# Prompt values taken for two heads in turn, later conditioning products, and half of the gate weights on another queue

## The reference

```python
def adaln_terms(c, w_ada, b_ada):
    mod = jax.nn.silu(c) @ w_ada + b_ada
    return tuple(m[:, None, :] for m in jnp.split(mod, 6, axis=-1))

def merge_branches(oa, ob, ga, gb, w_pa, w_pb, w_o):
    b, s = oa.shape[:2]
    ya = oa.reshape(b, s, A_OUT) @ w_pa
    yb = ob.reshape(b, s, B_OUT) @ w_pb
    return (ga * ya + gb * yb) @ w_o

def decoder_layer(x, c, pos, p, attend):
    sh1, sc1, gt1, sh2, sc2, gt2 = adaln_terms(c, p['w_ada'], p['b_ada'])
    h = rmsnorm(x, p['g_pre_mix']) * (1 + sc1) + sh1
    qa, ka, va, qb, kb, vb, logf, ga, gb = mixer_inputs(h, p['w_in'], p['b_f'], pos)
    oa, ob, state = attend(qa, ka, va, qb, kb, vb, logf)
    mix = merge_branches(oa.astype(x.dtype), ob.astype(x.dtype), ga, gb, p['w_pa'], p['w_pb'], p['w_o'])
    x = x + gt1 * rmsnorm(mix, p['g_post_mix'])
    h2 = rmsnorm(x, p['g_pre_ffn']) * (1 + sc2) + sh2
    ffn = hier_moe(h2, p['w_rg'], p['b_rg'], p['w_re'], p['b_re'], p['w_eg'], p['w_eu'], p['w_ed'])
    x = x + gt2 * rmsnorm(ffn, p['g_post_ffn'])
    return x, state
```

## Time and profile before

| | before |
| --- | --- |
| median of 3 runs | 1123.67 us (1120.25 to 1128.92) |
| the profiled execution | 1123.34 us, span 1121.2 us |
| PE busy (share of the span) | 984.8 us (88%) |
| VectorE / ScalarE / GpSimd busy | 384.2 / 206.1 / 186.8 us |
| DMA | 349.32 MB, mean 312 GB/s |
| mean granted TensorE clock | 0.949 |

### The profile page before, as it was taken

How to read it: one execution, slowest core, us unless ns; L and a number is a source line. 1 busy time by engine, 2 the same in 40 slices (tenths; PEclk the granted TensorE clock), 3 DMA queues, 4 the chain that set the end, 5 groups by cost and what they waited for, 6 DMA issues and landing times.

```text
span 1121.2 us, 17873 instructions
## 1 busy us (share of the span) xinstructions
PE 984.8 (88%) x7308; PEld 579.4 (52%) x7308; DVE 384.2 (34%) x889; ACT 206.1 (18%) x505; POOL 186.8 (17%) x210
## 2 busy tenths in 40 slices
PE   6999999998799999889999898699969997777860
PEld 4444444444467756666667565345545554444430
DVE  4200033215686373854057313115521320010005
ACT  4000000003354211002100212113312211111114
POOL 0000043302120103222230111000023332122110
PEclk9999999999899899989999999899969999899995
DMA  9997776687867699999999885997489999999956
GB/s 297 407 333 267 265 264 249 244 284 244 277 228 268 222 306 354 347 364 321 380 346 341 311 288 195 371 351 296 194 306 365 373 373 391 385 381 395 411 217 253
DMA packets 101805, 349.32 MB, mean 312 GB/s; under 512 B 11642, under 2 KB 59650, under 8 KB 82782
## 3 DMA queue, kind: packets, MB, share of 16 engines
q1 hardware_dynamic: 80414, 261.50, 65.1%
q0 software_dynamic: 15552, 79.97, 19.6%
q10 hardware_dynamic: 5760, 6.72, 1.9%
HBM read 336.31 MB, written 63.36 MB: 356 GB/s over the span
## 4 chain that ended last, share of the span: by engine, by line
PE 37%; DMA 22%; DVE 4%; issue 1%; ACT 1%; SPq 1%; DVEq 0%; POOLq 0%; ACTq 0%
DMA w_all<-in_w_exp 15%; PE bank L1665 9%; PE bank L2273 5%; PE bank L2104 5%; DMA w_all<-in_w_gates 3%; PE bank L1603 3%; PE bank L1657 2%; PE bank L1541 2%; PE bank L2124 2%; PE bank L1655 1%; DVE mods L1787 1%; PE bank L1526 1%; DMA turned<-in_w_o 1%; PE bank L1588 1%; PE bank L1569 1%
## 5 line engine op out<-in xcount | busy, mean ns | idle before, releaser
L1665 PE MATMUL bank<-turned,w_all 128*128 128x320 f32 (+1 forms) x512 | 145.0, 428 | 9.2 <-DMA w_all<-in_w_gates 3.9
L485 PE MATMUL bank<-w_all,turned 128*128 128x481 f32 (+2 forms) x384 | 120.3, 504 | 1.4 <-DVE turned L736 1.3
L485 PE MATMUL bank<-w_ring,turned 128*128 128x481 f32 (+2 forms) x384 | 118.4, 502 | 0.0
L1665 PEld LDWEIGHTS bank<-turned,w_all 128*128 128x128 f32 x512 | 95.0, 195 | 44.9 <-issue 20.0
L2104 PE MATMUL bank<-w_all,mix_row 128*64 128x256 f32 x736 | 95.2, 417 | 25.3 <-DMA w_all<-in_w_exp 24.3
L2104 PEld LDWEIGHTS bank<-w_all,mix_row 128*64 128x64 f32 x736 | 62.6, 151 | 64.8 <-issue 44.1
L1787 DVE STREAM_TRANSPOSE mods<-w_all 128x2048 f32<-128x2048 f32 (+1 forms) x39 | 86.3, 2236 | 22.2 <-PE bank L1541 9.1
L485 PEld LDWEIGHTS bank<-w_ring,turned 128*128 128x128 f32 (+1 forms) x384 | 57.2, 172 | 60.4 <-issue 57.3
L485 PEld LDWEIGHTS bank<-w_all,turned 128*128 128x128 f32 (+1 forms) x384 | 56.5, 172 | 61.6 <-issue 58.3
L2150 DVE COPY act_t<-bank 128x128 f32<-128x128 f32 x33 | 9.6, 291 | 199.4 <-PE bank L2114 197.7
L746 DVE COPY w_all<-bank 128x481 f32 (+5 forms) x32 | 16.9, 531 | 152.0 <-PE bank L485 151.8
(11 more groups left out here) (357 smaller groups left out, 1282.5 us busy)
## 6 DMA issues: line engine op xcount, KB each, us to landing
w_all<-in_w_exp SPq DMA_DIRECT2D x22, 2048.0 KB, 40.0
out_a_sample<-in_cache_a SPq DMA_DIRECT2D x8, 4080.0 KB, 21.9
w_all<-in_w_exp SPq DMA_DIRECT2D x25, 1024.0 KB, 37.6
mods<-in_w_ada SPq DMA_DIRECT2D x18, 1024.0 KB, 7.5
w_all<-in_cache_a SPq DMA_DIRECT2D x22, 512.0 KB, 7.3
turned<-in_w_exp SPq DMA_DIRECT2D x5, 2048.0 KB
mods<-in_w_exp SPq DMA_DIRECT2D x5, 2048.0 KB, 42.7
w_all<-in_cache_a SPq DMA_DIRECT2D x36, 256.0 KB, 5.8
```

Source lines behind the costliest of these rows:

```text
L485: mm = nc.tensor.matmul(m.banks[i][r:r + ROWS[i], 0:hi - lo], m.hT[:, k, i * P:i * P + ROWS[i]], ring[u][:, CW * k + lo:CW * k + hi], star ...
L1665: mm = nc.tensor.matmul(GATE[:, 0:WIDTH[h]], gate_w[b][k][:, c % 2 * P:(c % 2 + 1) * P], m.hT[:, k, 256 * h:256 * h + WIDTH[h]], start=k = ...
```

## The change

Three things change. In `weigh` of an A job the loop over the two heads becomes the innermost. The conditioning products, two of which lie ahead of the jobs, get none in the first three jobs, and the rest are spread over the other 21. In `phase_c` the first piece still runs ahead of step 0, but pieces 1 to 39 run one step later than before; and the second gate's weights of pairs 1 to 3 are loaded by ScalarE, at its step after the last reading piece, and no longer by SyncE.

```diff
-        OPENING = 2
-        pieces_at = lambda n: range(OPENING + (PIECES - OPENING) * n // N, OPENING + (PIECES - OPENING) * (n + 1) // N)
+        OPENING, FROM = 2, 3
+        upto = lambda n: OPENING + (PIECES - OPENING) * max(n - FROM, 0) // (N - FROM)
+        pieces_at = lambda n: range(upto(n), upto(n + 1))
...
-                    for b in range(2):
-                        h = 2 * p + b
-                        out = OUT[64 * b:64 * b + 64, i * P:(i + 1) * P]
-                        for x in range(min(i, 1) + 1):
-                            c = VA + HD * h
-                            nc.tensor.matmul(out, m.qkv[:, i - x, c:c + HD], pt[:, n % 2, b, x * P:(x + 1) * P], start=x == 0, stop=False)
-                        for g in range(2):
-                            for r in range(4):
-                                mm = nc.tensor.matmul(out[:, 32 * r:32 * r + 32], v_far[0:w, g, r, HD * h:HD * (h + 1)],
+                    out = [OUT[64 * b:64 * b + 64, i * P:(i + 1) * P] for b in range(2)]
+                    for x in range(min(i, 1) + 1):
+                        for b in range(2):
+                            c = VA + HD * (2 * p + b)
+                            nc.tensor.matmul(out[b], m.qkv[:, i - x, c:c + HD], pt[:, n % 2, b, x * P:(x + 1) * P], start=x == 0, stop=False)
+                    for g in range(2):
+                        for r in range(4):
+                            for b in range(2):
+                                h = 2 * p + b
+                                mm = nc.tensor.matmul(out[b][:, 32 * r:32 * r + 32], v_far[0:w, g, r, HD * h:HD * (h + 1)],
                                                       pt[0:w, n % 2, b, (2 + g) * P + 32 * r:(2 + g) * P + 32 * r + 32], start=False, stop=g == 1 and r == 3)
...
-    FIRST, END = 0, 82
+    FIRST, END = 1, 82
...
-        piece_at.setdefault(FIRST + n * (END - FIRST) // len(pieces), []).append(x)
+        piece_at.setdefault(FIRST + n * (END - FIRST) // len(pieces) if n else 0, []).append(x)
...
-                    for b in range(2):
-                        if t == step_of[("gate", 2 * p - 1, 1, b, 4)] + 1:
-                            gate_weights(p, b)
+                    if t == step_of[("gate", 2 * p - 1, 1, 0, 4)] + 1:
+                        gate_weights(p)
...
+            def gate_weights(p):
+                act.wait_ge(gate_pe, sum_of[(2 * p - 1, 1, 1)] + 1)
+                gate_weights_in(act, I, m, p, 1)
+
+            gates_at = {step_of[("gate", 2 * p - 1, 1, 1, 4)] + 1: p for p in range(1, PAIRS)}
...
+                if t in gates_at:
+                    gate_weights(gates_at[t])
```

More of the change, by code:

```diff
@@ L1420, in window @@
                 (window_keys_in if part == "k" else window_values_in)(sp, I, m.ring[slot_of[n]], arrived(n), own(u), g)
-            def gate_weights(p, b):
-                sp.wait_ge(gate_pe, sum_of[(2 * p - 1, 1, b)] + 1)
-                gate_weights_in(sp, I, m, p, b)
+            def gate_weights(p):
+                sp.wait_ge(gate_pe, sum_of[(2 * p - 1, 1, 0)] + 1)
+                gate_weights_in(sp, I, m, p, 0)
             def first_bias(u, x):
```

## The result

| | before | after |
| --- | --- | --- |
| median of 20 runs each | 1127.24 us (1120.25 to 1134.58) | 1121.76 us (1113.23 to 1133.12) |
| ratio after / before | | 0.9949, 95% interval 0.9930 to 0.9968 |
| the profiled execution | 1123.34 us, span 1121.2 | 1122.63 us, span 1120.4 |
| mean granted TensorE clock | 0.949 | 0.941 |

What follows compares the result with a forecast made beforehand. PE bounds the prompt attention, PE and DMA both the sample attention; expert weight loads then follow PE's handing back memory. From 1123.3 us, - 7 - 10.5 + 7 = 1112.8, rounded to 1112; range 1098 to 1122.

Steps and rivals of the forecast that it cites:

- the term of 17.5 us for parts 1 and 2: Prompt attention: gain of 10.5 us from alternating both heads' products and 7 us from later conditioning products.
- the 7 us of part 3: Sample attention: net loss of 7 us from the later pieces and moved gate weights; bounds gain 8.3, loss 22.
- What is won before 720 us should reach the end one for one: Before the experts' stage: expert weight loads start when PE hands memory back, so earlier gains reach the end in full.
- The factor of two: Prompt attention: alternating both heads' products halves their time, 3.25 to 1.6 us for a job with i=1.
- The wait of 4.87: Prompt attention: PE's 4.87 us wait for a conditioning weight block at 288.40 goes.
- The half clock after it: Prompt attention: half clock's 0.88 us share of the 16 records after PE's wait at 288.40 goes.
- the bounds of 5 to 8: Prompt attention: later conditioning products gain 7 us, at least 5 and at most 8.
- I expect the bias some 5 us earlier: Sample attention: the later step sends the page sums' reload ahead of 1 MB of gates, so bias comes 5 us earlier.
- the 2.59 us go: Sample attention: PE's 2.59 us wait at 462.54, behind VectorE's wait for the bias, goes.
- The stall of 3.89 us for the gates: Sample attention: PE's 3.89 us stall at 493.07 for the gate block issued at 456.63 goes, at best.
- The bias was to land at 509: Sample attention: on ScalarE's queue behind gates and merge weights, the bias lands at 509; VectorE wants it at 490.
- The wait for w_pb: Sample attention: PE waits for merge weights landing at 504.5, behind the gates at 43 packets per us; wanted at 493.7.

Runs made afterwards that it cites:

- gap_shift: Changed kernel with gate weights on SP's queue except the second pair's first block, plus repeats of one transpose at prompt job 16: 1112.9 us, ratio 0.9899.
- p12_old_c: Changed kernel with the old sample attention, so only the reordered products and later conditioning products against the kernel before: 1112.7 us, ratio 0.9906.
- p3_only: Kernel before with only the new sample attention (later pieces, second gate weights on ScalarE's queue) and the old prompt attention: 1129.8 us, ratio 1.0066.
- p1_turn: Kernel before with only the reordered `weigh`, both heads' products in turn: 1120.4 us, ratio 0.9980.

## Why the prediction was half right

**The step that failed.** It is the term of 17.5 us for parts 1 and 2. The prompt stretch is 92.8 to 95.4 us in the twelve kernels with both parts (gap_shift aside), and 108.8 and 106.6 in the two profiles with the old one: a gain of some 13.4 us between the means, 14.6 between the profiles of before and after. With that, and the 7 us of part 3 as forecast, the sum is -6.4 to -7.6, inside the measured 3.6 to 7.9. The 17.5 counted only what goes; it had nothing for the new wait of 1.10 us for a later block, for the half clock that stays, and for the gaps at "issue".

**What bounds the kernel.** "What is won before 720 us should reach the end one for one" is neither shown nor refuted. Parts 1 and 2 gave 10.6 us (7.0 to 14.3) at the end of 13 to 15 in the prompt attention. The one long wait behind it, 9.29 us, comes from the length of a way that differs by 6 us within one kernel. Whether a typical execution loses something there stays open. In the two profiles of before and after the sample attention loses 11.4 us and not 7; but these two differ by 0.7 us in time where the medians differ by 5.5, so they can't size that term.

**Part 1.** The factor of two is right: 3.25 us for a job with i=1 became 1.64 (1.6 forecast), and by the rows of PE the eight jobs give 10.6 us, against 10.8. The rule of the Trainium skill (TensorE: Matmul & The Clock Gate, "The mechanism"), by which a weight load overlaps only when its row group differs, would have given nothing. Here both heads use the same rows and differ in the output partitions alone, and the measurement decides. The stretch fell by 7.0 and 8.1 us only: 2.2 of it went into the gaps between instruction blocks (2.4 in the changed kernel), and the clock was 0.90 and 0.92 and not 0.94. Neither stood in the sum.

**Part 2.** The wait of 4.87 went, as forecast. The half clock after it mostly did not: L1037's 16 records still take 1.98 us at 286.06 (1.09 in p12_old_c), so that term was wrong. A wait of 1.10 us for a later block is new (308.04). Up to 323 us it gives 5.4 to 5.6, inside the bounds of 5 to 8 but not 7. That it gives only 2 to 3 us alone at the end goes with the clock near 365, which no step of mine had. That the clock was 0.98 with both parts is luck.

**Part 3, the step.** "I expect the bias some 5 us earlier" and "the 2.59 us go" were wrong: 2.12 us stayed at 451.65. The reload did go out ahead of the gates, but the write behind it, c_past, then stood behind them and took 12.8 us to land and not 7.7. From ScalarE's write to the first bias it is 30.0 us, as before (29.7). Whether the step guards against the long ways of 33.6 to 38.2 us, none of which stands in the six profiles with it, isn't settled by so few.

**Part 3, the queue.** Right in mechanism and place, and near in size. The stall of 3.89 us for the gates went. The bias was to land at 509 without the shift, 496 with the 12.7 us by which the sample attention begins earlier; VectorE got it at 493.76 and 497.82, after which PE had waited 9.54 us. Net loss forecast 7; measured 5 to 6 by the times of the changed kernel and p12_old_c, and 5.5 to 7.4 in p3_only. (The sample stretches differ by 7.0 us between the first two, but that is luck: both hold a wait of over 9 us, one of them in good part chance.) The wait for w_pb did not come in the changed kernel, since the queue sped up in the gathers' pauses. It came, at 501 to 504, in the three runs without these. My figure at 43 packets a us was 504.5 without the shift, some 492 with it, so there it came later still. That each queue gets a packet in turn (the Trainium skill, DMA: Bandwidth & Descriptors, "Queues, rings and completion order") agrees with these counts as long as both have work.

**The sum.** For -17.5 + 7 the runs show -13.4 to -14.6 in the stretch itself, -10.6 at the end, and +5 to +7. With 1112 predicted and 1121.8 measured the range just held, by its upper edge of 1122. I summed against a profiled execution that lies 3.9 us under the median of its kernel, and this is 3.9 of the 9.8 us between forecast and result.

## What to carry to other kernels

When an order gets denser, count what comes to the front as well as what goes: the next wait, the clock, the arrival of instructions. Before charging a gain against a chain of transfers, look whether the chain's start moves with the engine; here it did, to 0.01 us. And look at the same wait in two profiles of one kernel before giving it a cause: this one was 3.12 and 9.03 us. Order transfers by the time at which they are wanted, per queue: small ones that are wanted soon must not stand behind megabytes, and a queue that is empty then is the place for them. When one wait is mended, look at what its pause had let through.

## What the runs showed of the hardware

- Two matmul streams with the same rows and outputs in partitions 0 to 63 and 64 to 127, taken in turn, run in half the time: 3.25 to 1.64 us for a job with i=1.
- PE's instructions arrive in blocks of 16 KB, some 125 matmul records with their loads. At 6.4 to 6.8 us a block it stood 0.5 to 1.6 us at such a place in the changed kernel and p1_turn.
- An issue of two transfers on ScalarE's queue took 11.29 us in p3_only, with about 1,200 packets waiting on it, and held up everything behind it on ScalarE; with about 1,090 waiting it took 1.21 us in the changed kernel.
- Beside the gathers' 8 KB packets a queue of 1 KB packets moves 35 to 50 a us, without them up to 349.
- Where PE waits more in the sample attention it also gets less clock: 0.95 or 0.96 in the five kernels with 22.7 to 28.2 us of idle time in that stretch, 0.96 to 0.99 in those with 14.0 to 19.0.
